# Prompt attention by head pairs: two heads' scores and values in halves of the array, output born turned, probabilities scaled on GpSimd

## What is computed

```python
def forget_attend(q, q_idx, k, v, fk, fq):
    s = jnp.einsum('bqhd,bkhd->bhqk', q, k, preferred_element_type=jnp.float32) * (HEAD_DIM ** -0.5)
    s = s + (jnp.transpose(fq, (0, 2, 1))[..., :, None] - jnp.transpose(fk, (0, 2, 1))[..., None, :])
    mask = jnp.arange(k.shape[1])[None, :] <= q_idx[:, None]
    s = jnp.where(mask, s, NEG)
    p = jax.nn.softmax(s, axis=-1)
    return jnp.einsum('bhqk,bkhd->bqhd', p.astype(v.dtype), v)
...
            out = (o * jax.nn.silu(zg)) @ b_out_w[j]
```

## Time and profile before

| | |
|---|---|
| median of 3 runs | 2237.43 us (2235.73 to 2239.85) |
| profiled execution | 2240.53 us, span of its trace 2238.5 us |
| TensorE busy | 1975.8 us, 88% of the span |
| VectorE, ScalarE, GpSimd busy | 35%, 25%, 20% |
| mean granted TensorE clock | 0.94 of full speed |
| attention stage | from about 1359 to 2077 us of the span |

### The profile page before, as it was taken

One profiled execution on the slowest core, in us unless ns is written; L12 is line 12 of the kernel. 1 busy time (PEld: TensorE's weight loads), 2 busy tenths in 40 slices (PEclk: granted clock), 3 DMA queues, 4 the chain that ended last, 5 costly groups with the idle time before them and its releaser, 6 DMA issues. The chain is left out here.

```text
span 2238.5 us, 32246 instructions
## 1 busy us (share of the span) xinstructions
PE 1975.8 (88%) x12811; PEld 1656.0 (74%) x12811; DVE 793.5 (35%) x1318; ACT 564.8 (25%) x1155; POOL 441.4 (20%) x401
## 2 busy tenths in 40 slices
PE   6969999999979991499999996999999999998792
PEld 1259999999969991399999994666666666664691
DVE  0433150607140007621110004556565565553215
ACT  2112010201131113310000102444444444442232
POOL 0123323232212312532223322000000000000222
PEclk9989999999989995599999996999999999998896
DMA  7721212221161104134333225477777777766405
GB/s 269 253 77 43 69 61 76 63 68 59 51 221 48 38 19 176 32 93 128 95 80 108 89 71 177 171 247 231 270 262 235 264 264 236 263 217 226 137 20 176
DMA packets 231832, 318.10 MB, mean 142 GB/s; under 512 B 39921, under 2 KB 165474, under 8 KB 230923
## 3 DMA queue, kind: packets, MB, share of 16 engines
q1 hardware_dynamic: 199891, 270.39, 37.4%
q10 hardware_dynamic: 31664, 45.57, 5.6%
q0 software_dynamic: 128, 0.07, 0.0%
HBM read 270.35 MB, written 45.63 MB: 141 GB/s over the span
## 5 line engine op out<-in xcount | busy, mean ns | idle before, releaser
L121 PE MATMUL ps<-actH,w_hi_a 128*128 128x352 f32 x960 | 210.5, 327 | 3.4 <-DVE w_lo_a L92 3.4
L121 PE MATMUL ps<-actH,w_lo_a 128*128 128x352 f32 x960 | 208.1, 324 | 0.0
L121 PE MATMUL ps<-actL,w_hi_a 128*128 128x352 f32 x960 | 207.5, 324 | 0.0
L121 PE MATMUL ps<-actH,w_hi_c 128*128 128x352 f32 x792 | 173.5, 327 | 20.9 <-DVE w_lo_c L92 20.9
L121 PE MATMUL ps<-actH,w_lo_c 128*128 128x352 f32 x792 | 171.6, 324 | 0.0
L121 PE MATMUL ps<-actL,w_hi_c 128*128 128x352 f32 x792 | 171.4, 325 | 0.0
L1370 PE MATMUL ps<-kT,qT 64*128 64x512 f32 (+3 forms) x384 | 160.5, 526 | 7.7 <-ACT PT_short L1524 4.0
L121 PEld LDWEIGHTS ps<-actH,w_hi_a 128*128 128x128 f32 x960 | 163.5, 190 | 3.9 <-DVE w_lo_a L92 3.7
L121 PEld LDWEIGHTS ps<-actH,w_lo_a 128*128 128x128 f32 x960 | 165.8, 189 | 0.0
L1396 PEld LDWEIGHTS ps<-ident,K 128*128 128x128 f32 x1024 | 112.6, 143 | 71.0 <-issue 48.6
L121 PEld LDWEIGHTS ps<-actL,w_hi_a 128*128 128x128 f32 x960 | 163.9, 189 | 0.0
(11 more groups left out here) (241 smaller groups left out, 3116.6 us busy)
## 6 DMA issues: line engine op xcount, KB each, us to landing
K<-in_cache_k_dram SPq DMA_DIRECT2D x128, 512.0 KB, 4.8
V<-in_cache_v_dram SPq DMA_DIRECT2D x128, 512.0 KB, 4.0
adaw<-in_ada_w_dram SPq DMA_DIRECT2D x12, 2048.0 KB, 8.6
w_raw_a<-in_a_in_w_dram SPq DMA_DIRECT2D x32, 512.0 KB
g_d<-g ACTq DMA_DIRECT2D x16, 528.0 KB, 2.7
mov_b<-g_d SPq DMA_DIRECT2D x16, 528.0 KB, 5.5
w_raw_b<-in_a_out_w_dram SPq DMA_DIRECT2D x16, 512.0 KB
w_raw_c<-in_kv_w_dram SPq DMA_DIRECT2D x16, 512.0 KB
```

Source lines behind the costliest of these rows:

```text
L121: mm = pe.matmul(acc[:, c, 0:CH], wt[:, j % SPL, k, :], act[:, k0 + k, c * CH:(c + 1) * CH], start=first and k == 0 and s == 0, stop=last ...
```

## The change

Prompt attention is now done for both heads of a pair at once, in 32 "rounds of rows" R of four steps each (k = 0 to 3). One R takes a long and a short block of queries, LONG with 8-i key blocks and SHORT with i+1 (i = R mod 4), nine together, cut into three chunks of at most four blocks: widths 4, 4-i and i+1.

- `scores(R+1, k)`: one matmul per head and chunk, the first head in rows 0 to 63 of the array and bank 0, the second in rows 64 to 127 and bank 1. Both banks are used again for the next chunk as soon as VectorE has read them.
- `values(R, k-1)`: the probabilities are now the moving operand and the values (64 columns) the weights; the first head goes to partitions 0 to 63 and the second to 64 to 127. The output comes out turned, so `o_tok`, its transposes and `normalise` are gone; VectorE multiplies it with the gate once per R (`gate`).
- The probabilities are multiplied by 1/row sum before they are transposed, in place, on GpSimd (`tensor_scalar`, four per R).
- `turn_probs` uses the single bank 2, a head at a time.
- A sample's 1/row sum is applied to its output on ScalarE instead of to its 2080 probabilities on VectorE; its maximum is taken page group by page group (`pmax`); its new rows' scores become side work at step 0 of a round.
- `VR` is 4 instead of 6. The pair's loads are cut in two (`qk` with both `nF`, and `zv`), with other due times.
- Before the loop, VectorE does the logits and maxima of the first R, and only then fills `qblk`, for which PE waits.

```diff
-VR = 6
+VR = 4
...
+                for R in range(RN):
+                    for u in (LONG, SHORT):
+                        at = row(R, u)
+                        pool.wait_ge(s_bias, 6 * R + (4 if u == LONG else 6))
+                        blk = Sb[:, R % 2, :, at.stop - P:at.stop]
+                        pool.affine_select(out=blk, in_=blk, compare_op=ALU.is_ge, fill=NEG, base=0,
+                                           pattern=[[0, 2], [-1, P]], channel_multiplier=1).then_inc(s_mask, 1)
+                    for u in (LONG, SHORT):
+                        pool.wait_ge(s_rinv, 2 * R + u + 1)
+                        for h in range(2):
+                            t = Sb[:, R % 2, h, row(R, u)]
+                            pool.tensor_scalar(t, t, rinv[:, R % 2, u, h:h + 1], None, ALU.mult).then_inc(s_scaled, 1)
...
+                def scores(R, c):
+                    i, b0, w, _ = chunk(R, c)
...
+                    if 3 * R + c:
+                        pe.wait_ge(s_bias, 2 * (3 * R + c))
+                    for h in range(2):
+                        hs = slice(h * HD, (h + 1) * HD)
+                        mm = pe.matmul(ps[:, h, 0:w * P], qT[hs, p % 2, i * P:(i + 1) * P],
+                                       kT[hs, p % 2, b0 * P:(b0 + w) * P], start=True, stop=True)
                     mm.then_inc(s_S, 1)
...
+                def turn_probs(R, c, h):
+                    i, b0, w, at = chunk(R, c)
+                    pe.wait_ge(s_scaled, 4 * R + 2 * (c // 2) + h + 1)
...
+                    for j in range(w):
+                        for h in range(2):
+                            hs = slice(h * HD, (h + 1) * HD)
+                            mm = pe.matmul(ps[hs, 5, col:col + P], Vt[:, p % 2, b0 + j, hs], PT[:, n % 2, h, j * P:(j + 1) * P],
+                                           start=b0 + j == 0, stop=b0 + j == i)
                     mm.then_inc(s_O, 1)
...
+                    if R < RN and k < 3:
+                        turn_probs(R, k, 0)
+                    if R + 1 < RN and k < 3:
+                        scores(R + 1, k)
...
+                    if R < RN and k:
+                        values(R, k - 1)
+                    if R < RN and k < 3:
+                        turn_probs(R, k, 1)
+                    if side_work(s):
+                        side(s, *side_work(s))
...
+                    if R + 1 < RN and k == 2:
+                        exps(R + 1, LONG, 0)
+                    if R + 1 < RN and k == 3:
+                        exps(R + 1, LONG, 1)
+                        exps(R + 1, SHORT, 0)
+                        exps(R + 1, SHORT, 1)
...
+                    if R + 1 < RN and k < 3:
+                        logits(R + 1, k)
...
+                    if R + 1 < RN and k == 2:
+                        row_max(R + 1, LONG)
+                    if R + 1 < RN and k == 3:
+                        row_max(R + 1, SHORT)
+                        invert(R + 1, LONG)
...
+                for c in range(3):
+                    logits(0, c)
+                    if c:
+                        row_max(0, c - 1)
+                dve.wait_ge(s_set, 64)
+                for h in range(2):
+                    for c in range(2):
+                        r, at = slice(h * HD, (h + 1) * HD), (2 * c + h) * NT
+                        dve.tensor_copy(qblk[r, c::2, :, at:at + NT],
```

More of the change, by code:

```diff
@@ L1191, in stage_attention, with blocks, chunk, row @@
         STEPS = PAGES + V0 + 1
-        G_OUT, G_PTD, G_PTN, G_OS = (2, 3), (4, 7, 8, 9), 5, 6
+        RN = NP * QB // 2
+        LONG, SHORT = 0, 1
+        G_NS, G_PTD, G_PTN, G_OS = 0, (4, 7, 8, 9), 5, 6
         NGR = NPG // KG
-        def unit(u):
-            return u // UN, u % UN // QB, ORDER[u % QB]
-        def s_bank(u):
-            return ps[:, 2, :] if u % 2 == 0 else ps[:, 0:2, :].rearrange("p b n -> p (b n)")
+        def blocks(R):
+            p, i = R // 4, R % 4
+            return p, (QB - 1 - i, i)
+        def chunk(R, c):
+            p, (iL, iS) = blocks(R)
+            if c < 2:
+                return iL, 4 * c, (4 if c == 0 else iL - 3), 4 * c * P
+            return iS, 0, iS + 1, (iL + 1) * P
+        def row(R, u):
+            p, i = blocks(R)
+            return slice(0, (i[0] + 1) * P) if u == LONG else slice((i[0] + 1) * P, NBLK * P)
         def side_work(s):
@@ L1207, in side_work @@
                 return None
-            if g in G_OUT and r < NP:
-                return "out", r, G_OUT.index(g)
+            if g == G_NS and r < NB:
+                return "score", r, 0
             if g in G_PTD and r < NB:
@@ new lines, in values @@
+                def values(R, c):
+                    i, b0, w, _ = chunk(R, c)
+                    p, n = R // 4, 3 * R + c
+                    pe.wait_ge(s_PTe, 2 * n + 2)
+                    if R % 4 == 0 and c == 0:
+                        pe.wait_ge(s_zv[p % 2], 32 * (p // 2 + 1))
+                    if c == 0 and R:
+                        pe.wait_ge(s_gate, R)
+                    col = P if c < 2 else 0
+                    for j in range(w):
+                        for h in range(2):
+                            hs = slice(h * HD, (h + 1) * HD)
+                            mm = pe.matmul(ps[hs, 5, col:col + P], Vt[:, p % 2, b0 + j, hs], PT[:, n % 2, h, j * P:(j + 1) * P],
+                                           start=b0 + j == 0, stop=b0 + j == i)
@@ L1444, in side @@
                         pe.wait_ge(s_side_read, sides_before[s])
-                    if what == "out":
-                        pe.wait_ge(s_On, UN * (r + 1))
-                        for i in range(4):
-                            mm = pe.transpose(ps[:, 6, i * P:(i + 1) * P], o_tok[:, r % 2, 4 * part + i, :],
-                                              ident[:, :])
+                    if what == "score":
+                        for c in range(NP // HG):
+                            for q in range(HG):
+                                k = q * (NP // HG) + c
+                                mm = pe.matmul(ps[q * QUAD:(q + 1) * QUAD, 6, 0:NS], qblk[:, k, r, :], k_s[:, k, :],
+                                               start=c == 0, stop=c == NP // HG - 1)
                     elif what == "sample":
@@ L1562, in _, with logits @@
                                   ALU.add).then_inc(s_X, 1)
-                dve.wait_ge(s_set, 64)
-                for h in range(2):
-                    for c in range(2):
-                        r, at = slice(h * HD, (h + 1) * HD), (2 * c + h) * NT
-                        dve.tensor_copy(qblk[r, c::2, :, at:at + NT],
-                                        q_s[r, c::2, :].rearrange("p k (b t) -> p k b t", t=NT)).then_inc(s_qst, 1)
+                def logits(R, c):
+                    i, b0, w, at = chunk(R, c)
+                    p = R // 4
+                    dve.wait_ge(s_S, 3 * R + c + 1)
+                    if R >= 2 and c == 0:
+                        dve.wait_ge(s_PT, 6 * (R - 1))
+                    if R % 4 == 0 and c == 0:
+                        dve.wait_ge(s_nF[p % 2], 32 * (p // 2 + 1))
+                    for h in range(2):
+                        dve.scalar_tensor_tensor(out=Sb[:, R % 2, h, at:at + w * P],
+                                                 in0=nF[:, p % 2, h, b0 * P:(b0 + w) * P],
+                                                 scalar=Ftok[:, i, 2 * p + h:2 * p + h + 1], in1=ps[:, h, 0:w * P],
+                                                 op0=ALU.add, op1=ALU.add).then_inc(s_bias, 1)
@@ L1622, in _ @@
-                logits(0)
-                row_max(0)
-                for s in range(STEPS):
-                    r, g, work = s // UN - 1, s % UN, side_work(s)
-                    if s > KG and s % KG == 1 and s <= PAGES + 1:
-                        page_rows(s // KG - 1)
-                    if s + 1 < NU:
-                        logits(s + 1)
-                    if 2 <= s < NU + 2 and s % 2 == 0:
-                        normalise(s - 2)
+                invert(0, LONG)
+                for s in range(STEPS):
+                    R, k = s // 4, s % 4
+                    r, work = s // UN - 1, side_work(s)
```

292 lines of the change are left out of this document (126 added, 166 removed).

## The result

The changed kernel takes **2312.52 us**, median of 4 runs (2312.13 to 2314.21), against 2236.58 us (2234.29 to 2239.85, 4 runs) for the kernel before on the same chip: ratio 1.033, 95% interval 1.032 to 1.034. It is slower, as forecast, and inside the range; but the loss is 76 us where 30 were forecast. It lies where rival (c) had put it (2308).

The account below looks back on a forecast made before the run. TensorE's queue was taken to set the pace, busy 80.7 of 82.9 us a round. Work 62.8, waits 17 and clock 5.5 made 85.3; start +14, second round +2.7, six rounds +14.4, tail -2 gave 2267 us, range 2205 to 2325.

Parts of the forecast that it names:

- rival (c): GpSimd's scaling of probabilities costs what the two-input operation does: 5.2 us more a round, 2308 us; chance 0.12.
- TensorE's work: In the attention loop, two heads side by side halve scores and values: 62.8 us a round, from a counted 80.
- The step that failed: GpSimd's scaling of 1024 probability columns priced at the one-input cast's 1.04 us, upper bound 2.49 us.
- The clock term: TensorE's clock halves after idle pieces in the loop: 2.3 falls at about 2.4 us, 5.5 us a round.
- Rival (b): TensorE's clock stays up in the loop: a round of 79.8 us, 2227 us in all; chance 0.25.
- The waits: TensorE idles in the loop for page copies and scaled probabilities: 17 us a round, where 2.2 were.
- By boundary: TensorE's waits between one R and the next: 5.0, 3.5, 1.8 and 2.7 us for i = 0 to 3.
- side work and new rows: The next page waits for ScalarE's copies behind side work and VectorE's new rows: 3.8 us a round.
- the issue of a DMA: On ScalarE, between the sample's exponent and the copy of page k = 3: an estimated 0.3 us.
- (d): The two heads' array halves do not overlap: some 12 us more a round, 2360 us; chance 0.06.
- The ends: Outside the steady loop: first page at about 1392, page 4 at about 1412, start +14 us, tail -2 us.
- `VR` 4: Four value buffers are free in the loop as long as a value page lands within four steps (20 us).

Follow-up runs that it names:

- the kernel with four key pages: Changed kernel with scaling on VectorE, later sample exponent, forget-term loads spread, side work before the second head's transposes, and `KR` 4 instead of 3: 2172.5 us.
- the constant factor: Changed kernel with GpSimd multiplying by 1.0 instead of 1/row sum, waits as before: 2308.1 us, one run.
- six intermediate kernels: Changed kernel with scaling on VectorE and later sample exponent, alone or with exponents together, spread loads, side work first or idle transposes: 2210.7 to 2233.65 us.

## Why the prediction was right in sign and wrong in size

A whole round by the prediction's three terms. The measured ones are TensorE's work at full clock (its busy time in the kernel with four key pages and a clock of 1.00, which differs from the changed one in order and not in products), its idle time, and what is left of its busy time:

| us a round | work | waits | clock | sum |
|---|---|---|---|---|
| forecast | 62.8 | 17 | 5.5 | 85.3 |
| changed kernel, mean of rounds 3 to 7 | 65.3 | 18.5 | 8.3 | 92.1 |

**The step that failed** is "For the scaling I take the one-input cast, 1.04 us for 1024 columns; the two-input subtraction at 2.49 us is the upper bound". It measured 2.84 us, above the bound even; the prediction had named "over 2 us" as a sign of being wrong. At the four boundaries of a round that is some 1.8, 1.6, 1.4 and 1.2 us more than the cast's rate (8, 7, 6 and 5 blocks, 2.84 to 1.88 us against 1.04 to 0.65), together 6.1 us a round, on the path. Both operations had been in the profile, and the choice between them rested on the number of inputs alone. A price between ends so far apart should have moved the forecast toward the middle, or the chance of (c) well above 0.12. Shown by moving the operation (-89 us) and by the constant factor.

Rival (c), with 5.2 a round and 0.12 chance, had the mechanism, and was right to 5 us in the whole. That closeness is partly luck: its sum, 90.5 us a round, has 4 us too much of other waits, and 2.5 too little work and 2.8 too little clock.

**The clock term**, 5.5 us, was too small. The prediction counted 2.3 falls a round at 2.4 us each. The trace has three in each of rounds 3 and 4 and four from then on, one at each boundary; in the round shown the four cost 8.2 us (73.5 - 65.3), 2.1 each. So the price of a fall was about right and their number was not: at the boundaries of i = 1 (a wait of 2.33 us) and i = 2 (1.74) the clock fell too. With the scaling on VectorE there are one or two falls a round, and the same subtraction gives 68.9 - 65.3 = 3.6 us: with a cheap scaling the term would have been too large. Rival (b), the clock staying up, came true only where waits were filled or gone.

**The waits**, 17 us forecast, measured 18.8 in the round shown, but not for the reasons given. By boundary, with forecasts in brackets: i = 0 5.4 us (5.0), i = 1 4.0 (3.5, both with the waits for `ogs` and `PTd` just before), i = 2 2.4 (1.8), i = 3 3.9 (2.7), and side work and new rows 3.1 (3.8). Of the 18.8, transposes that wait for GpSimd are 3.02 + 2.33 + 2.33 + 1.74 = 9.4. Without the scaling's excess of 6.1 only 12.7 are left, each of the five smaller than forecast by 0.6 to 1.2; the kernel with scaling on VectorE agrees (12.7 us of idle time in a round). So the other waits had been put some 4 us too high, which hid two thirds of the scaling's error. The order of events in the chain had been followed well (for i = 0 the maximum was done at 4.7 us where 4.6 was said, and the page waited 3.09 for 3.5); the issue of a DMA, put at 0.3 us, ran beside the exponent and delayed nothing. With a cheap scaling the kernel is at 2224, 43 us below the forecast: the other waits had been put 4.3 us a round too high and the clock 1.9.

**TensorE's work** was put at 62.8 us a round and measures 65.3, where the old round's count of 80 stood against 80.7. So 15.4 us of work were removed, not 17.2; which product or change of shape has the 2 us was not followed up. The halves overlap, so (d) falls. The busy time over all rounds came to 117.7 us for scores of all widths, where below 110 was said, and to 84.1 for values, where below 80 was said. The scores of 512 columns have 83.6 of it at a mean of 962 ns. That is not a dearer product but a clock that is often at half in this place: in the kernel with four key pages the mean is 713 ns. That TensorE's busy time fell by 60 us only is due to the clock: 15.4 us less work a round and 8.3 us more for the half clock leave 7.1, or 57 in eight rounds.

**The ends** came out well: first page at 1388.0 (1392), page 4 at 1409.3 (1412), start +13, tail -3. `VR` 4 was costed at nothing in the loop, and it costs nothing there; alone it costs the kernel before 5 us, behind the last page.

**Not settled:** how much of the six intermediate kernels' loss is the late pages themselves and how much the clock that falls behind them, and where the 2 us of uncounted work lie.

## What to carry to other kernels

Price an operation by the same instruction on the same engine; where the trace has none, take the gap between the nearest rows as part of the forecast, above all if the operation is on the path. That an engine is idle for 78 of 83 us says nothing of what an operation costs there, and for work that stands between two other engines the cost decides: moving 2.8 us to the busier VectorE, where it took 0.75, gave 89 us. When TensorE's work is cut, a gap can cost twice, once as a wait and again in the clock (18.5 us of gaps a round came with 8.3 us lost to the half clock), but it need not: in the kernel with four key pages 7.8 us of gaps a round left the clock at 1.00. Rings that had been deep enough for the old pace (here three key pages) become the next limit: the same change, with the scaling on VectorE, a shorter chain and a fourth page, is 3% faster than the kernel before.

## What the runs showed of the hardware

VectorE and GpSimd held each other up. The beginning of the stage in the changed kernel, in order of time:

```profile
1369.75 5.23 DVE L1647 TENSOR_TENSOR_SCAN B<-one,B 128x2052 f32<-128x2052 f32 x1 [0.87 <-ACT B L1511]
1370.77 6.01 POOL L1346 TENSOR_SCALAR_AFFINE_SELECT mpre<-mpre 128x1920 f32<-128x1920 f32 x1
1375.01 2.85 DVE L1649 TENSOR_SCALAR B<-B 128x2048 f32<-128x2048 f32 x1
...
1387.21 0.74 DVE L1661 COPY qblk<-q_s 64x128 f32<-64x128 f32 x4
```

and in the kernel before, where the select is over ahead of the scan:

```profile
1370.16 2.01 POOL L1336 TENSOR_SCALAR_AFFINE_SELECT mpre<-mpre 128x1920 f32<-128x1920 f32 x1
1372.42 4.43 DVE L1572 TENSOR_TENSOR_SCAN B<-one,B 128x2052 f32<-128x2052 f32 x1
1376.89 1.29 DVE L1574 TENSOR_SCALAR B<-B 128x2048 f32<-128x2048 f32 x1
```

Side by side the select takes 6.01 us instead of 2.01, the scan 5.23 instead of 4.43, the multiplication on VectorE 2.85 instead of 1.29. All fifteen traces of the changed kernel and its variants show these times within 0.01 us. The ends fit two engines that take turns rather than share a rate: the scan ends at 1374.98, the select 1.8 us later, which is about what it takes alone, and the multiplication 1.1 us after the select. The four copies of `qblk`, 4.19 us beside GpSimd's selects before, take 0.74 alone; two of the four had taken 1.97 and 1.93 us, each until the select beside it was over, and the other two 0.21 and 0.22. So of those 4.19 us, which the prediction took as their price, some 3.4 were waiting for the other engine. The Trainium skill ("GPSIMD Engine Reference", section 8) says that GpSimd shares its interfaces to SBUF with VectorE and contends with those of its instructions that run in a two-port mode or have two inputs in SBUF. These rows agree that the two contend; they don't show the modes. GpSimd's scaling shows nothing of it: its 16 operations on 1024 columns lie between 2.83 and 2.85 us. But beside those VectorE ran only copies out of PSUM and reciprocals of two columns, so they test little.
